# Seven products for eight in a projection of a hybrid decoder layer on eight cores

## The chip, the cores and the metric

The kernel runs on all 8 cores of one Trainium2 chip. Each core computes one prompt sequence of 2064 positions and 16 of the 128 sample tokens, 2080 tokens in all, with its own copy of the weights; the cores don't exchange anything. The metric is the device time of the slowest core in microseconds, as the median of several runs.

## The reference, cut to what matters

```python
def trunk_layer(x, ...):                       # x (B, T, 1024)
    h = rmsnorm(x, g_pre_mix)
    z = h @ w_in                               # 1024 -> 4096
    u, v, bg, cg, ga, gb = split(z)            # 512, 512, 512, 512, 1024, 1024
    a = multiscale_pool(u) @ w_pool * scale    # trailing means over 2, 4, 8, 16 tokens
    b = (bg * causal_dwconv(cg * v)) @ w_conv_out
    merged = sigmoid(ga) * a + sigmoid(gb) * b
    x = x + rmsnorm(merged @ w_o, g_post_mix)  # w_o: 1024 x 1024, the projection of the change
    h = rmsnorm(x, g_pre_ffn)
    gate, val = split(causal_dwconv(h @ w_up)) # 1024 -> 5632, 3 taps
    y = (silu(gate) * val) @ w_down            # 2816 -> 1024
    return x + rmsnorm(y, g_post_ffn)
```

The sample tokens go through the same layer with carried states (15 pooling rows, 2 convolution rows, 2 rows of the up-projection). All is float32 in DRAM; the matmuls take bfloat16 operands.

## The kernel before, in words

Activations lie transposed: channels on the 128 partitions, tokens along the free axis. Everything lies in one SBUF tensor `big`, and buffers are ranges of it that are used again by later stages. The first stage (mixer) cuts the 2080 tokens into five tiles, 512 and four times 392 (`TA`, index t = 0 to 4). The second (FFN) cuts them into 448, 464, 448, 448, 256 (`TB_N`).

For each mixer tile the kernel does, in program order: F, sixteen blocks of 8 matmuls for u, v, B and C (`F_block`, order `FSEQ`) with the convolution (`conv_c`, L666 and L669) and the pooling (`pool_c`, L697, L703) on VectorE; B, eight times two gates of 8 matmuls (`gates`, L804) and a merge of 1 + 4 matmuls (`merge`, L817, L821, L823), whose result is `MERGED[t]`; the projection `WO(t)`, eight groups of 8 matmuls with 392 columns, each evacuated by ScalarE twice (`wo_evac`: scaled by g_post_mix into `R[t]`, L834, and squared into `XSQ2[t]`, L836). Then `epi(t)`: a tree of additions (L602) and a matmul with ones give the mean square, ScalarE makes its inverse root (L611, L614); `epi_r` multiplies R by it (L864), adds x by an accumulating DMA issued from GpSimd (L570), squares (L872) and stores x to yT (L566, from SyncE's queue); `epi_n2` makes the second norm and `epi_x` (L888) writes h2, which goes to DRAM. `prenorm(t+1)` makes h of the next tile (L628, L640).

The work overlaps between tiles. Before the change the program order is B(0), WO(0), epi(0), B(1), then for t = 2 and 3: F(t), prenorm(t+1), WO(t-1), epi(t-1), B(t); then F(4) with WO(3) and epi(3) after its fifth block, B(4), WO(4). R, XSQ2, X and MERGED have one place each for all tiles (tile 0's are wider but begin at the same word), so a tile's R can be written only when its predecessor's readers, the products L888 and the yT stores, are through.

PSUM has 8 banks. Bank 7 is for norm sums, the other seven go round in program order (`next_bank`): a group of matmuls waits until the group seven banks earlier is evacuated.

The order on each engine is static. `Sched` records every operation with its tokens (ranges of SBUF in steps of 4 words, banks), keeps TensorE's in program order except the norm sums, and orders the other engines by a model of durations: the priority of an operation is the time at which TensorE's first operation that depends on it is due. The model gives each engine its own durations and knows of no influence of one engine's work on another's. All instructions then run in that order, with waits on semaphores. L559 issues every matmul.

The down-projection of the second stage already uses seven products for eight (`wdown`, with sums on GpSimd by `sumb`, L998, and bank additions on VectorE, L1056). `pre_ffn` prepares the sample tokens' share of the FFN convolution: a load of 704 KB and three products of 704 elements on GpSimd (L1190, L1192, L1194), in the period of tile 2.

## Time and profile before

| | |
|---|---|
| median of 3 runs | 798.0 us (797.36 to 799.73) |
| profiled execution, in all | 798.55 us |
| its span on the slowest core (core 2) | 797.0 us |
| spans of the 8 cores | 792.7 to 797.0 us |
| mean granted TensorE clock | 0.996 to 1.000 of 2.4 GHz |
| TensorE, VectorE, ScalarE, GpSimd busy | 98%, 73%, 55%, 41% |

A busy time is the union of an engine's instructions. Matmuls overlap in the pipeline and their ends are modelled, so the pace of a row of matmuls is the distance of their starts and not their duration. Times within the execution are counted in us from the start of the span. The mixer's periods, as far as the change touches them, lie at 144.8 to 205.4 us (F(2), WO(1), B(2)), 205.4 to 266.0 us (F(3), WO(2), B(3)) and 266.0 to 329.7 us (F(4), WO(3), B(4)); the last projection follows to about 338.5 us, and then the second stage begins.

### The profile page before, as it was taken

The numbers are of one execution on the slowest core, as the hardware profiler recorded it, in microseconds if no ns is written. First come the engines' busy times: TensorE is split into PE (matmuls) and PEld (weight loads), VectorE is DVE, ScalarE is ACT, GpSimd is POOL, SyncE is SP. The second block draws the span as 40 slices with busy tenths as digits, with TensorE's granted clock in tenths as the row PEclk, the third lists the DMA queues.
The fourth block names the chain that finished last, engine by engine and source line by source line (L and its number), as shares of the span: only waits on it lengthen the run. The fifth ranks groups of instructions, "written<-read, shape, count | busy, mean of one in ns | idle before, by whom it ended". The sixth has DMA issues, their size and how long they took to land.

```text
span 797.0 us, 16162 instructions; the slowest of 8 cores (792.7 to 797.0 us)
## 1 busy us (share of the span) xinstructions
PE 781.9 (98%) x4902; PEld 476.0 (60%) x4906; DVE 584.8 (73%) x1035; ACT 440.7 (55%) x998; POOL 326.0 (41%) x311
## 2 busy tenths in 40 slices
PE   6999999999999999999999999999999999999997
PEld 5445445555555555555554545577665777579984
DVE  1898438797886857578889839875679667885686
ACT  2433274675656545576676434754458534775562
POOL 6433001004001124559734312596556483494422
PEclk9999999999999999999999999999999999999999
DMA  9999813946303889999984787894535856258774
GB/s 181 196 164 151 131 52 98 211 100 156 117 22 67 194 150 196 175 149 159 127 194 159 146 145 240 273 186 149 172 109 77 193 179 186 60 109 253 232 226 155
DMA packets 82628, 124.35 MB, mean 156 GB/s; under 512 B 5584, under 2 KB 62544, under 8 KB 82528
## 3 DMA queue, kind: packets, MB, share of 16 engines
q0 software_dynamic: 38992, 43.14, 38.3%
q1 hardware_dynamic: 43552, 80.17, 33.5%
q8 instruction: 42, 0.69, 0.4%
q14 instruction: 42, 0.34, 0.2%
HBM read 117.40 MB, written 36.24 MB: 193 GB/s over the span
## 4 chain that ended last, share of the span: by engine, by line
PE 91%; DMA 3%; DVE 2%; issue 2%; ACT 1%; SPq 1%; DVEq 0%; ACTq 0%
PE ps L559 91%; DMA w_dns<-big 2%; DMA big<-xT 1%; DVE big L942 1%; SPq L566 0%; ACT big L938 0%; DVE big L1115 0%; DVE big L494 0%; DVE big L602 0%; ACT big L1228 0%; ACT big L628 0%; DVE big L1177 0%; DVEq L1390 0%; DVE big L759 0%; ACT ps L932 0%
## 5 line engine op out<-in xcount | busy, mean ns | idle before, releaser
L559 PE MATMUL ps<-big 128*128 128x392 bf16 (+10 forms) x4902 | 781.9, 323 | 9.9 <-ACT big L1228 4.7
L559 PEld LDWEIGHTS ps<-big 128*128 128x128 bf16 x4906 | 476.0, 98 | 315.4 <-issue 13.7
L942 DVE SCALAR_TENSOR_TENSOR big<-ps,big 128x448 f32<-128x448 f32 (+2 forms) x440 | 252.0, 636 | 85.1 <-ACT big L935 67.1
L952 POOL TENSOR_TENSOR big<-big 128x448 bf16<-128x448 f32 (+2 forms) x110 | 128.6, 1177 | 156.9 <-ACT big L951 102.3
L938 ACT ACTIVATE big<-ps,big 128x448 f32<-128x448 f32 (+2 forms) x220 | 126.9, 600 | 14.2 <-PE ps L559 5.4
L951 ACT ACTIVATE big<-big 128x448 f32<-128x448 f32 (+2 forms) x110 | 60.0, 546 | 67.2 <-DVE big L942 65.5
L998 POOL TENSOR_TENSOR big<-big 128x896 bf16<-128x896 bf16 (+3 forms) x45 | 87.9, 2010 | 20.5 <-PE ps L559 14.7
L570 POOL DMA_DIRECT2D big<-xT x16 | 15.3, 962 | 129.6 <-DVE big L817 116.8
L804 ACT ACTIVATE big<-ps 128x392 f32<-128x392 f32 (+1 forms) x80 | 38.9, 511 | 51.4 <-DVE big L823 26.7
L572 POOL DMA_DIRECT2D big<-w_up x44 | 31.4, 719 | 56.3 <-PE ps L559 51.5
L602 DVE TENSOR_TENSOR big<-big 128x1568 bf16<-128x1568 bf16 (+3 forms) x28 | 22.2, 794 | 38.6 <-ACT big L836 28.1
L932 ACT ACTIVATE ps<-big 128x4 f32<-128x4 f32 (+1 forms) x98 | 17.2, 175 | 53.8 <-PE ps L559 53.3
L817 DVE SCALAR_TENSOR_TENSOR big<-ps,big 128x392 f32<-128x392 f32 (+1 forms) x40 | 25.8, 644 | 27.5 <-PE ps L559 27.4
L572 POOL DMA_DIRECT2D big<-w_in x32 | 23.1, 733 | 21.1 <-DMA big<-w_in 11.5
L834 ACT ACTIVATE big<-ps,big 128x392 f32<-128x392 f32 (+1 forms) x40 | 24.3, 608 | 12.7 <-PE ps L559 12.6
L697 DVE TENSOR_TENSOR big<-big 128x406 f32<-128x406 f32 (+7 forms) x50 | 29.7, 596 | 1.5 <-ACT big L719 0.4
L1056 DVE TENSOR_TENSOR big<-big,ps 128x448 f32<-128x448 f32 (+1 forms) x48 | 28.1, 618 | 0.2 <-PE ps L559 0.2
L669 DVE SCALAR_TENSOR_TENSOR big<-big 128x392 f32<-128x392 f32 (+1 forms) x40 | 25.2, 642 | 2.9 <-ACT big L666 2.5
L640 DVE SCALAR_TENSOR_TENSOR big<-big 128x392 bf16<-128x392 f32 (+1 forms) x40 | 24.2, 646 | 3.7 <-ACT big L617 3.7
L888 DVE SCALAR_TENSOR_TENSOR big<-big 128x392 bf16<-128x392 f32 (+1 forms) x40 | 25.2, 674 | 1.5 <-ACT big L614 1.5
L872 ACT ACTIVATE big<-big 128x784 bf16<-128x784 f32 (+1 forms) x20 | 17.8, 892 | 14.8 <-DMA big<-xT 12.5
L823 DVE TENSOR_TENSOR big<-big 128x392 bf16<-128x392 f32 (+1 forms) x40 | 23.6, 599 | 1.9
(79 smaller groups left out, 423.2 us busy)
## 6 DMA issues: line engine op xcount, KB each, us to landing
big<-w_dns SPq DMA_DIRECT2D x30, 704.0 KB, 5.5
big<-w_up POOLq DMA_DIRECT2D x44, 256.0 KB, 13.5
big<-w_dnb SPq DMA_DIRECT2D x16, 704.0 KB, 5.1
big<-w_in POOLq DMA_DIRECT2D x32, 256.0 KB, 22.9
big<-xT POOLq DMA_DIRECT2D x16, 392.0 KB, 8.7
big<-w_dn POOLq DMA_DIRECT2D x8, 704.0 KB, 11.5
w_dnb<-big SPq DMA_DIRECT2D x8, 704.0 KB, 7.3
big<-xT SPq DMA_DIRECT2D x6, 784.0 KB, 7.2
```

Source lines behind the costliest of these rows:

```text
L559: ins = e.matmul(o, lhsT=l, rhs=x, start=(start and i == 0), stop=(stop and i == last))
L572: return S.add("pool", lambda e: e.dma_start(out=out, in_=in_, max_dma_last_dim=mx), r, w, dma=True, byts=byts, pri=pri, after=after)
L669: dve(lambda e, k=k: e.scalar_tensor_tensor(out=cv, in0=p[:, 2 + k + lo:2 + k + N], scalar=cc(C_WC + 4 * k + c), in1=cv, op0=ALU.mult, op1 ...
L697: dve(lambda e, nx=nx, cur=cur, s=s, a2=a2: e.tensor_tensor(out=nx[:, a2:W], in0=cur[:, a2:W], in1=cur[:, a2 - s:W - s], op=ALU.add), [ct] ...
L804: act(lambda e, b=b, g=g: e.activation(out=GT[t].ap[:, g, lo:N], in_=bank(b, N, lo), func=AF.Sigmoid), [("ps", b)], [GT[t].t(g, 1)], N, ps ...
L817: dve(lambda e: e.scalar_tensor_tensor(out=A_, in0=bank(bp, N, lo), scalar=cc(C_PS + m), in1=A_, op0=ALU.mult, op1=ALU.mult), [("ps", bp), ...
L938: act(lambda e, b=b, fj=fj, tt=tt: e.activation(out=tt[:, 0:n], in_=bank(b, n), func=AF.Copy, scale=cc(C_WF + fj)), [("ps", b), KCST], [to ...
L942: dve(lambda e, b=b, fj=fj, tt=tt, k=k: e.scalar_tensor_tensor(out=tt[:, 0:n], in0=ps[:, b * 512 + k:b * 512 + k + n], scalar=cc(C_WF + 44 ...
L951: silu[0] = act(lambda e: e.activation(out=g, in_=g, func=AF.Silu), [T.t(0, 1)], [T.t(0, 1)], n, tab="silu")
L952: prod[0] = S.add("pool", lambda e: e.tensor_tensor(out=gb.ap[:, q, 0:n], in0=g, in1=v, op=ALU.mult), [T.t()], [("sb", gb.off + q * gb.cw, ...
L998: pool_tt(lambda e, i=i, k=min(FH, i + 4): e.tensor_tensor(out=out[:, i:k, :], in0=gap(t, p0, h0)[:, i:k, :], in1=gap(t, p1, h1)[:, i:k, : ...
L1056: dve(lambda e: e.tensor_tensor(out=o, in0=o, in1=src, op=op), [("ps", b)] + tk, tk, N)
```

## The change

Tiles "2 to 4" of the change are t = 1, 2, 3. Write W for w_o in quarters (two halves of the input channels by two of the output channels) and M for MERGED in quarters (input channels by halves of the 392 tokens). `WO(t)` with its eight products of quarters becomes fourteen steps (`wo_step`: seven products A to G, two halves `md` of the output rows each). A step is 8 matmuls of 196 columns into one bank. F and G are copied out of the bank by ScalarE, twice each with opposite signs; the others are added to R in place by VectorE, once or twice. R is no longer scaled by g_post_mix in the evacuation; `epi_r` does it for t = 1 to 3 with eight products in place of four wider ones. The squares are taken from R after the last additions.

The steps are spread over F of the next tile (`F_with_WO`, table `WOAT`): from block 5 on in F(2), 3 in F(3) and 1 in F(4), the last four together after block 15 in F(2), two in F(3). The sums of M (five a tile, 784 elements, `wo_sum`) go to GpSimd. The sums of W are made once on chip by GpSimd (`wo_sums`, 21 instructions), partly in place of W's quarters, partly in gaps between buffers. As W's quarters B and E are overwritten, the last tile (`WO_last`) is computed from the sums F and G, the quarters D and C, and differences of MERGED's rows (eight subtractions on VectorE): as many matmuls of 392 columns as before, in another order, with four banks open at first in place of three.

To make room, `pre_ffn` moves to the second stage (third tile) in five chunks through the small buffer XB, each a load, three products on GpSimd and a store, and some buffers move by a few words.

```diff
@@
+    def wo_sums():
+        for o, p, q, op in (("F", "E", "C", ALU.add), ("G", "D", "B", ALU.add), ("B", "B", "C", ALU.subtract),
+                            ("A", "D", "C", ALU.add), ("E", "D", "E", ALU.subtract)):
...
+    MSUM = {"A": ((0, 0), (1, 1), ALU.add, MA), "B": ((1, 0), (1, 1), ALU.add, MB), "C": ((1, 0), (0, 0), ALU.subtract, (1, 0)),
+            "D": ((1, 1), (0, 1), ALU.subtract, MC), "E": ((0, 0), (0, 1), ALU.add, (0, 1))}
+    MRHS = {"A": MA, "B": MB, "C": (1, 0), "D": MC, "E": (0, 1), "F": (0, 0), "G": (1, 1)}
...
+    def wo_sum(t, p):
+        q0, q1, op, o = MSUM[p]
+        (a0, t0), (a1, t1) = mq(t, q0), mq(t, q1)
+        out, tk = mq(t, o) if isinstance(o, tuple) else (o.ap[:, :, 0:NA // 2], [o.t()])
+        pool_tt(lambda e: e.tensor_tensor(out=out, in0=a0, in1=a1, op=op), t0 + t1, tk, 2 * NA)
+
+    def wo_step(t, p, md):
+        h = NA // 2
+        r = MRHS[p]
+        rhs, rt = mq(t, r) if isinstance(r, tuple) else (r.ap[:, :, 0:h], [r.t()])
+        b = next_bank()
+        for mi in range(2):
+            w, wt = w_k(p, 2 * md + mi)
+            pe([(bank(b, mi * h + h, mi * h), w[k], rhs[:, k, :]) for k in range(4)], wt + rt, [("ps", b)], h)
...
+        for r2, half, op in {"F": ((4, 0, 1.0), (4, 1, -1.0)), "G": ((0, 1, 1.0), (0, 0, -1.0)),
+                             "A": ((0, 0, ALU.add), (4, 1, ALU.add)), "B": ((0, 0, ALU.add),),
+                             "C": ((0, 0, ALU.add), (4, 0, ALU.add)), "D": ((0, 1, ALU.subtract), (4, 1, ALU.subtract)),
+                             "E": ((4, 1, ALU.subtract),)}[p]:
+            o, tk = y(r2, half)
+            if p in "FG":
+                act(lambda e, o=o, op=op: e.activation(out=o, in_=src, func=AF.Copy, scale=op), [("ps", b)], tk, NA, psum=True)
+            else:
+                dve(lambda e, o=o, op=op: e.tensor_tensor(out=o, in0=o, in1=src, op=op), [("ps", b)] + tk, tk, NA)
...
+    WOSTEPS = [(p, md) for p in "FGBCDAE" for md in range(2)]
+
+    WOAT = {2: (5, 6, 7, 8, 9, 10, 11, 12, 13, 14, 15, 15, 15, 15), 3: (3, 4, 5, 6, 7, 8, 9, 10, 11, 12, 13, 14, 15, 15), 4: (1, 2, 3, 3, 4, 4, 5, 5, 6, 6, 7, 7, 8, 8)}
+
+    def F_with_WO(t):
+        for p in "BDA":
+            wo_sum(t - 1, p)
+        for i in range(16):
+            F_block(t, i)
+            if t == L and i < 9:
+                wup(1)
+            for x in [x for x, at in enumerate(WOAT[t]) if at == i]:
+                wo_step(t - 1, *WOSTEPS[x])
+                if x == 3:
+                    wo_sum(t - 1, "C")
+                    wo_sum(t - 1, "E")
+                if x == 13 and t == L:
+                    epi(L - 1)
+
+    def WO_last(hook):
...
+        ms = (4, 5, 6, 7)
+        bs = {m: next_bank() for m in ms}
+        for d, k0, k1 in ((0, 0, 4), (1, 0, 3), (1, 3, 4)):
+            for m in ms:
+                part(bs[m], m, d, k0, k1)
+        for m in ms:
+            wo_evac(t, bs[m], m)
+            hook()
...
@@
     epi(0)
+    wo_sums()
     B(1)
     load_states()
-    pre_ffn_load()
     for t in range(2, L):
-        for i in range(16):
-            F_block(t, i)
+        F_with_WO(t)
         load_x(t + 1, 2)
         prenorm(t + 1)
-        WO(t - 1)
         epi(t - 1)
-        if t == 2:
-            pre_ffn()
         B(t)
...
+    F_with_WO(L)
     small_states()
     B(L)
-    WO(L, split=True, hook=lambda: wup(1))
+    WO_last(lambda: wup(1))
     load_h2(0)
...
@@
+            if t == 2 and j % 4 == 1 and j < 20:
+                chunk = pre_ffn(j // 4)
+            if t == 2 and j % 4 == 3:
+                pre_ffn_sum(*chunk)
```

## Rows read from the trace of the kernel before

**Rows 1.** The page: the span, and busy time (share of the span) and count.

```profile
span 797.0 us, 16162 instructions; the slowest of 8 cores (792.7 to 797.0 us)
...
PE 781.9 (98%) x4902; PEld 476.0 (60%) x4906; DVE 584.8 (73%) x1035; ACT 440.7 (55%) x998; POOL 326.0 (41%) x311
```

**Rows 2.** Waits of TensorE, longest in total: in all, times, longest.

```profile
PE ps L559 <- ACT big L1228: 4.7, 2, 3.7
...
PE ps L559 <- DVE big L602: 1.3, 1, 1.3
```

**Rows 3.** Busy (x) of PE, PEld, DVE, ACT, POOL; then PEclk, DMA share, GB/s.

```profile
144.80:205.40 60.60, 60.60 (x367) 35.70 (x366) 49.04 (x86) 39.20 (x73) 8.55 (x7) 1.00 0.70 166
205.40:266.00 60.60, 60.60 (x367) 35.75 (x366) 45.83 (x82) 36.08 (x70) 3.49 (x4) 1.00 0.28 69
266.00:329.70 63.70, 63.03 (x381) 37.02 (x379) 48.07 (x103) 32.57 (x58) 22.12 (x32) 1.00 0.99 171
```

**Rows 4.** Groups by shape: busy us, mean ns of one, idle us before.

```profile
L559 PEld LDWEIGHTS ps<-big 128*128 128x128 bf16 x4906 | 476.0, 98 | 315.4 <-issue 13.7
L559 PE MATMUL ps<-big 128*128 128x392 bf16 x1464 | 245.2, 329 | 2.2 <-DVE big L602 1.3 <-ACT big L804 0.7 <-DVE big L778 0.2
...
L559 PE MATMUL ps<-big 128*128 128x224 bf16 x616 | 63.3, 259 | 0.0
```

**Rows 5.** Groups by shape, on ScalarE and VectorE.

```profile
L834 ACT ACTIVATE big<-ps,big 128x392 f32<-128x392 f32 x32 | 18.9, 591 | 12.7 <-PE ps L559 12.6
L640 DVE SCALAR_TENSOR_TENSOR big<-big 128x392 bf16<-128x392 f32 x32 | 18.8, 621 | 0.0
...
L821 DVE TENSOR_TENSOR big<-ps,big 128x392 f32<-128x392 f32 x32 | 17.9, 560 | 1.3 <-PE ps L559 0.8
```

**Rows 6.** Groups by shape: the sums on GpSimd.

```profile
L998 POOL TENSOR_TENSOR big<-big 128x896 bf16<-128x896 bf16 x20 | 38.3, 1923 | 12.8 <-PE ps L559 12.4
...
L998 POOL TENSOR_TENSOR big<-big 128x672 bf16<-128x672 bf16 x10 | 16.8, 1682 | 0.3
```

**Rows 7.** Timeline of VectorE: start, duration, instruction, idle before.

```profile
184.56 1.16 DVE L823 TENSOR_TENSOR big<-big 128x392 bf16<-128x392 f32 x1
...
188.25 0.55 DVE L821 TENSOR_TENSOR big<-ps,big 128x392 f32<-128x392 f32 x1
188.72 1.46 DVE L864 TENSOR_TENSOR big<-big 128x784 f32<-128x784 f32 x1
190.11 0.55 DVE L823 TENSOR_TENSOR big<-big 128x392 bf16<-128x392 f32 x1
190.59 0.96 DVE L864 TENSOR_TENSOR big<-big 128x784 f32<-128x784 f32 x1
```

**Rows 8.** Timeline of GpSimd at the same place.

```profile
183.91 1.37 POOL L1190 TENSOR_TENSOR big<-big 128x704 f32<-128x704 f32 x1 [42.67 <-PE ps L559]
185.43 1.53 POOL L1192 TENSOR_TENSOR big<-big 128x704 f32<-128x704 f32 x1
187.11 2.25 POOL L1194 TENSOR_TENSOR big<-big 128x704 f32<-128x704 f32 x1
```

**Rows 9.** Timeline of VectorE in F(2).

```profile
147.81 0.57 DVE L765 TENSOR_TENSOR big<-ps,big 128x392 f32<-128x392 f32 x1 [0.96 <-PE ps L559]
...
162.98 0.73 DVE L888 SCALAR_TENSOR_TENSOR big<-big 128x498 bf16<-128x498 f32 x1
...
165.28 3.97 DVE L888 SCALAR_TENSOR_TENSOR big<-big 128x498 bf16<-128x498 f32 x6
```

**Rows 10.** Timeline of SyncE's queue in F(2).

```profile
152.02 0.38 SPq L566 DMA_DIRECT2D yT<-big  x1
```

**Rows 11.** DMA issues at 151.5 to 165 us: count, KB, us to landing.

```profile
yT<-big SPq DMA_DIRECT2D x1, 996.0 KB, 9.5
```

**Rows 12.** Busy us of each engine near the start, with the granted clock.

```profile
8.00:12.80 4.80, 1.15 (x17) 0.88 (x15) 0.88 (x2) 1.06 (x1) 0.70 (x1) 0.96 1.04 206
12.80:16.20 3.40, 3.36 (x21) 2.37 (x22) 0.88 (x2) 1.06 (x1) 3.40 (x7) 0.56 1.12 228
```

More of the change, by code:

```diff
@@ L389, in build_nc @@
     al.o = o_sq2 + KC * NMX // 2
[L390 to L391 removed]
+    XB = Buf(SBW - 128 - 512, 8, 64)
+    al.o = XB.end
     ST_CONV = al(4, 2 * NS)
[L393 removed]
     X = per_tile(KC, False, [o_x, W_O.off] + [o_cv + 5 * NA + 32] * 3)
@@ L456, in build_nc @@
     PRE = Buf(h2b.off + 800, 44, NS)
-    PREW = Buf(ST_CONV.off - 44 * NS, 44, NS)
     H2, G = [h2a, h2b], [g0, g1]
-    ST_FFN = Buf(h2b.off, 44, 2 * NS)
-    assert ST_FFN.end <= PREW.off and PRE.end <= h2b.end <= ST_CONV.off
+    assert PRE.end <= h2b.end <= ST_CONV.off
     TAIL = Buf(h2b.off, 1, 44 * 18)
@@ new lines, in WO_last, with part @@
+    def WO_last(hook):
+        t, lo = NTA - 1, 0
+        mg = MERGED[t]
+        for i in (1, 0):
+            for k in range(4):
+                dve(lambda e, k=k, i=i: e.tensor_tensor(out=DB[i][k].ap[:, 0, :], in0=mg.ap[:, 4 * i + k, :], in1=mg.ap[:, 4 - 4 * i + k, :],
+                                                        op=ALU.subtract), [mg.t(k, 1), mg.t(4 + k, 1)], [DB[i][k].t()], NA, rate=2.0)
+        def part(b, m, d, k0, k1):
+            r = m // 4
+            w, wt = w_k(("DC" if d else "GF")[r], m % 4)
+            xs = [(DB[r][k].ap[:, 0, :], DB[r][k].t()) if d else (mg.ap[:, 4 - 4 * r + k, :], mg.t(4 - 4 * r + k, 1)) for k in range(4)]
+            pe([(bank(b, NA), w[k], xs[k][0]) for k in range(k0, k1)], wt + [xs[k][1] for k in range(k0, k1)], [("ps", b)], NA,
+               start=d == 0 and k0 == 0, stop=d == 1 and k1 == 4)
+        ms = (4, 5, 6, 7)
[6 more added lines that the diff above has]
+            hook()
+        for m in range(4):
+            b = next_bank()
+            part(b, m, 0, 0, 4)
+            part(b, m, 1, 0, 4)
+            wo_evac(t, b, m)
+            hook()
@@ L863, in epi_r @@
         r = R[t].ap[:, k:k + 2, lo:N]
-        tt(lambda e: e.tensor_tensor(out=r, in0=r, in1=SD.ap[:, rs, lo:N].unsqueeze(1).to_broadcast([128, 2, N - lo]),
-                                     op=ALU.mult), [R[t].t(k, 2), SD.t(rs, 1)], [R[t].t(k, 2)], 2 * N)
+        for x in range(k, k + 2) if 0 < t and not last else ():
+            dve(lambda e, x=x: e.scalar_tensor_tensor(out=R[t].ap[:, x, :], in0=R[t].ap[:, x, :], scalar=cc(C_G2 + x),
+                                                      in1=SD.ap[:, rs, 0:N], op0=ALU.mult, op1=ALU.mult),
+                [R[t].t(x, 1), SD.t(rs, 1), KCST], [R[t].t(x, 1)], N, stt=True)
+        if t == 0 or last:
+            tt(lambda e: e.tensor_tensor(out=r, in0=r, in1=SD.ap[:, rs, lo:N].unsqueeze(1).to_broadcast([128, 2, N - lo]),
+                                         op=ALU.mult), [R[t].t(k, 2), SD.t(rs, 1)], [R[t].t(k, 2)], 2 * N)
         if last:
@@ L1340, in build_nc @@
         if t == NTB - 1:
-            sp_dma(PRE.flat, pre_d, ["pre"], [PRE.t()], 128 * 44 * NS * 4, pri=-15000.0)
+            sp_dma(PRE.flat, pre_d, [("pre", 10 * c) for c in range(5)], [PRE.t()], 128 * 44 * NS * 4, pri=-15000.0)
         for j in range(FC):
```

94 lines of the change are left out of this document (63 added, 31 removed).

## The prediction

> **What bounds the kernel now.** I read the page's header and busy lines first, then the list of waits on TensorE, then the busy sums by stage, and last the timelines around two places. The page: TensorE is busy 781.9 of 797.0 us [rows 1], and its waits are 4.7 us behind the first evacuations at the start, and then single ones of up to 1.3 us [rows 2]. So the kernel is bound by the number of matmul columns: a column taken away is time gained, as long as no other engine becomes late. The next view says how near that is. In the three periods that the change touches (F of a tile, the projection before it, B of that tile) the sums show TensorE without a gap but for 0.67 us [rows 3], and VectorE busy 49.0 of 60.6, 45.8 of 60.6 and 48.1 of 63.7 us [rows 3]. Its room is 11.6, 14.8 and 15.6 us. GpSimd is nearly idle there, apart from DMA issues and the three state products that the change moves away.
>
> **The change part by part.**
>
> *Matmuls.* Matmuls overlap, so their mean duration is not their pace. A matmul of 392 columns lasts 329 ns; the period of 60.60 us holds 367, two of them cut by its edges, which is 166 ns each [rows 3, 4]. The difference, 163 ns, is the modelled end, so 224 columns (259 ns) go at 96 ns. That gives 0.417 ns a column, and 196 columns go at 84 ns. A projection was 64 x 0.166 = 10.6 us and becomes 14 steps x 8 = 112 x 0.084 = 9.4 us: 1.2 us less a tile, 3.5 us for tiles 1 to 3 (the diff's index). The last tile keeps 8 x 8 matmuls of 392 columns, so it gains nothing. Its first four banks finish together after 32 matmuls instead of three after 24, which moves ScalarE's evacuation, not TensorE. I cost that at 0, to at most 1 us if the differences come late behind the last merge.
>
> The Trainium skill speaks against this term: "TensorE: Matmul & The Clock Gate", section LDWEIGHTS, gives a weight load of 128 columns 128/1.2 = 107 ns. If loads set the pace, 112 of them would take 12.0 us, and three tiles would get slower by 4 us. The trace has a mean load of 98 ns [rows 4] and matmuls with a load each at 96 ns, so loads at least overlap down to that pace. Below it nothing is shown. If the pace stuck at 96 ns, the projection would take 10.8 us and the change would lose 0.4 us on three tiles; that is the bound I keep.
>
> *VectorE.* Added per tile: 2 x (2 + 1 + 2 + 2 + 1) = 16 additions of a bank (steps A to E), each like L821's 392 columns from PSUM. That one lasts 560 ns, but the next starts 0.48 us later (188.25 to 188.72) [rows 5, 7]: 7.7 us. The normalisation becomes 8 products like L640 (620 ns, about 0.54 apart) in place of 4 of 784 elements (about 0.9 apart): +0.8 us. So +8.5 us a period, while the period shrinks by 1.2. The room left is 1.9, 5.1 and 5.9 us. ScalarE loses 16 evacuations (591 ns for L834's [rows 5]) and gets 8 copies and 4 squares of double width, about as much: 0. The eight bf16 differences of the last tile are 8 x 0.3 to 0.5 us, beside TensorE's first 16 matmuls: 0.
>
> *GpSimd.* New: 20 weight sums of 512 elements (one in two pieces), and 5 sums of 784 elements a tile. L998 takes 1.68 us in the mean at 672 elements and 1.92 at 896, waits for VectorE within it included [rows 6]: I take 1.7 us for 784 and 1.2 for 512. F's and G's sums have only the weights and tile 0's freed buffers to wait for; B's and E's wait for the projection of tile 0, and A's for the squares of tile 0, whose room they take. So about 4 x 1.2 + 5 x 1.7 = 13.3 us of GpSimd fall into F of tile 2, 8.5 us into F of tiles 3 and 4, and 9.6 us into B of tile 1. GpSimd has the time. Behind a sum that waits for the last merge stand, in F of tile 4, issues of w_up loads, which are first used 232 matmuls (38 us) after F: 0. The question is what the sums do to VectorE. Three GpSimd products stand alone in the mixer, at 183.91, 185.43 and 187.11 us [rows 8]. The merge L823 beside the first, with two inputs in SBUF, took 1.16 us where its next takes 0.55, and L864 beside the third took 1.46 us where its next takes 0.96; L821, which reads PSUM, kept its 0.55 us beside the same product [rows 7]. So 5.2 us of GpSimd cost VectorE 1.1 us, where VectorE had gaps anyway. In F nearly two thirds of VectorE's work (convolution, pooling, h, h2, the trees) is of the kind with two SBUF inputs, and it runs without gaps. The bounds are 0.2 us of VectorE per us of GpSimd, as in these rows, and 1.0, if every sum meets a waiting instruction. I take 0.6, between them: nearer to the upper end than the row, since F has no gaps, and below it, since a third of the work is not of that kind. That costs VectorE 8.0 us in tile 2's period and 5.1 in each of the other two; 1.1 us comes back because the state products leave. The balance is 1.9 + 1.1 - 8.0 = -5.0, then 0.0 and +0.8 us.
>
> The Trainium skill, "SBUF", section Who interferes with whom, has the same thing as a rule: a VectorE instruction with two SBUF inputs and a GpSimd one that reads SBUF exclude each other, and the second waits for the whole of the first. By this rule, the trace agrees: L823 ended 0.4 us after the product did.
>
> *R and its readers.* The sums of tile t-1 are written into R by ScalarE (F and G) and added to by VectorE. R has one place for all tiles. Before, the projection came after all of F, so R had 21 us more to come free. Now F's first copy into rows 4 and 5 comes after block 5 of tile 2. F of tile 2 starts near 145.0: its second block ended when L765 started at 147.81 [rows 9], less two blocks of 1.33 us. Step F ends at 145.0 + 6 x 1.33 + 0.67 = 153.7. Seven banks rotate, two a block, so block 9 wants F's bank at 153.7 + 3 x 2.0 = 159.7. But the copy waits for the y store of tile 0's rows 4 to 7, issued at 152.02 and 9.5 us under way [rows 10, 11], and for the last products with h2's scale, which VectorE made from 162.98 to 169 us with nothing urgent behind them [rows 9]. The store alone puts the copy at 161.5 and block 9 at about 162.5 us: a wait of 3 us. ScalarE stands behind that copy too, with the v and u evacuations queued after it. This wait and VectorE's shortage of 5.0 fall together, since VectorE catches up while TensorE waits, and the banks let it be late by some 6 us. For tile 2 I take 3.5 us. Tiles 3 and 4 have the same reuse at blocks 3 and 1, with smaller stores behind: 0 to 2.5 us each, I take 0.75.
>
> *The rest.* The sample state's products move into the second stage: 15 small GpSimd products and 10 small DMAs over 20 pairs. That is the 5.1 us of the old ones spread out, on an engine busy 41% of the span [rows 1]; if a product of a pair comes later by 0.5 us, a bank's rotation covers it: 0. The h2 buffer moves by 64 words, and load_h2(1) now waits for the last projection: it is needed 22 pairs of 16 matmuls later. On SP nothing due sooner is behind it: 0, up to 1 us.
>
> **The sum.** -3.5 + 3.5 + 0.75 + 0.75 = +1.5 us. The profiled execution spans 797.0 and took 798.55 us in all; the median is 798.0. The forecast is 798.0 + 1.5 = 799.5 us. What this kernel's measurement can tell from no change is about 0.3%, 2.4 us: below 795.6 is faster, above 800.4 slower.
>
> **The rivals.**
> 1. *The columns come out whole* (0.22). The early copy is ordered well, R comes free sooner because its readers are now urgent, and GpSimd's price is the lower one, 0.2: balances 0.3, 3.4 and 4.2 us, all positive. Waits under 1.2 us in all; 794.5 to 795.7, best 795. For it: TensorE waits nearly nowhere before, with the same seven banks. Against: the store's landing is in the rows.
> 2. *VectorE becomes the bound* (0.25, the slower side). At 1.0 us per us, the balances are -10.3, -3.4 and -2.6 us, 16 us short; the banks and the work that can slip hide some of it once. Waits of 8 to 13 us, so 803 to 808 us, middle 805. It decides when GpSimd costs VectorE over 0.75 of its own time: then the second and third period are short too, by 1.3 and 0.5 us. For it: no gap in F; against: 0.2 in the only burst there. A gap in one piece can also cost clock: after a stretch in which TensorE was busy 1.15 of 4.8 us, the granted clock was 0.56 over the next 3.4 us [rows 12], which is 1.7 us more.
> 3. *Short matmuls don't go at 84 ns* (0.05). At 96 to 107 ns the columns give nothing or cost up to 4 us; with the waits above, 803 to 808.
>
> The forecast itself has 0.48, with waits of 2 to 8 us: 796.5 to 802.5. That the change doesn't do what it says has no part: the count of matmuls and columns stands in the diff.
>
> **How the numbers follow.** Faster: rival 1, 0.22. Slower by over 0.3%: rivals 2 and 3, and the upper quarter of the forecast's own case, 0.25 + 0.05 + 0.10 = 0.40. Within 0.3%: 0.38. The forecast's own range is 796.5 to 802.5; for 8 in 10 it reaches from 794.6 into rival 2's middle, 805.5.
>
> **What would show it.** Right: matmuls of 196 columns about 84 ns apart; in F of tile 2 a wait of TensorE for ScalarE or VectorE of about 3 us near 160 us; VectorE busy over 95% in F; its two-input instructions lengthened beside GpSimd's sums and the PSUM ones not. Wrong: if TensorE runs through F of tile 2 without a wait, rival 1 holds; if waits of several us stand in all three periods, rival 2.

## The result and the profile after

The changed kernel takes 814.95 us (814.06 to 817.02, 6 runs) against 797.72 us (6 runs) for the kernel before: 1.0217 times as long, 95% interval 1.0201 to 1.0233. That is 17.2 us slower. The forecast was 799.5 us, with a range from 794.6 to 805.5. Ratios and intervals, here and below, are of executions in which no die ran at a lowered clock.

The page of the changed kernel, on its slowest core (core 2); its lines answer to [rows 1].

```profile
span 815.5 us, 16715 instructions; the slowest of 8 cores (805.8 to 815.5 us)
...
PE 784.6 (96%) x5046; PEld 487.1 (60%) x5050; DVE 635.2 (78%) x1103; ACT 437.7 (54%) x993; POOL 379.9 (47%) x359
```

TensorE's busy time has hardly changed. What is new is waiting. The list of waits, for [rows 2] (columns: in all in us, times, longest in us); L922 is step F's copy into R, L819 the gates, L617 the trees, L877 the weight sums.

```profile
PE ps L574 <- ACT big L922: 10.4, 2, 5.3
...
PE ps L574 <- DVE big L617: 3.4, 3, 1.6
PE ps L574 <- ACT big L819: 2.6, 2, 1.7
...
PE ps L574 <- POOL big L877: 1.0, 1, 1.0
```

The three periods on the same core, for [rows 3], cut at the first matmul of F(2), F(3), F(4) and the last projection (columns as there):

```profile
145.90:210.70 64.80, 60.56 (x418) 38.95 (x416) 60.02 (x105) 35.91 (x67) 18.40 (x13) 1.00 0.50 101
210.70:278.60 67.90, 62.43 (x419) 40.07 (x417) 59.89 (x102) 36.16 (x67) 12.61 (x9) 0.95 0.32 81
278.60:346.10 67.50, 62.43 (x418) 40.47 (x417) 59.42 (x118) 30.75 (x53) 27.81 (x35) 0.95 0.77 139
```

They sum to 200.2 us; cut at the same matmuls, the kernel before took 184.0. The slowest core is not the typical one: in F(3) it waited 5.3 us in one piece, where the longest wait of the other seven was 1.2 to 1.9 us. Core 5 waited least of all, so what it shows is the part that the cores had in common. Its periods, and its waits between 110 and 345 us:

```profile
144.40:208.50 64.10, 60.71 (x417) 38.83 (x416) 60.57 (x105) 36.31 (x68) 20.39 (x13) 1.00 0.40 107
208.50:270.50 62.00, 60.32 (x418) 39.05 (x416) 59.05 (x102) 35.36 (x67) 12.74 (x9) 1.00 0.31 77
270.50:338.30 67.80, 62.74 (x418) 40.72 (x416) 59.34 (x118) 30.64 (x53) 27.72 (x35) 0.95 0.78 145
```

```profile
PE ps L574 <- ACT big L922: 7.8, 5, 5.1
PE ps L574 <- ACT big L819: 3.0, 3, 1.9
PE ps L574 <- DVE big L617: 0.2, 1, 0.2
```

And the 6.8 us around the end of its wait of 5.1 us, which ended at 285.7 us, on core 5, with TensorE's granted clock (the last column but two):

```profile
284.60:291.40 6.80, 5.68 (x28) 4.01 (x29) 6.39 (x13) 4.53 (x11) 0.24 (x1) 0.50 0.96 187
```

TensorE was granted half its clock for 6.8 us, from 1.1 us before the wait's end. It was busy 5.68 of them, so that costs 5.68 / 2 = 2.8 us. "The mixer", in all that follows, is the stretch from the first pair of 392-column matmuls behind 100 us to the first matmul of the second stage. That pair is a norm sum inside WO(0), some 7 us ahead of B(1). The account of core 5 over this stretch closes: measured from the distances of matmul starts, delays over 0.3 us are 12.4 us (the list above has 11.0 of them, as it leaves the first part of each wait out), half clock 2.8, fewer columns -3.5, together +11.7; the stretch is 239.9 us where the kernel before has 228.1, +11.8. On the other cores the delays, measured so, are 12.6 to 16.8 us; the median of the eight is 14.4.

Over the eight cores, as medians: the start up to that pair took 108.7 us before and 110.0 after, the mixer 228.1 and 241.4, the rest 457.2 and 458.9. So 13.3 us lie in the mixer; +1.3 and +1.7 lie ahead of it and behind it. These are medians of cores in one execution each, while the 17.2 us are of the slowest core over all executions, so they sum to 16.3 and not to 17.2.

Now the place of the longest wait, in F(4) on core 2. VectorE (start, duration, instruction, idle before), then GpSimd, ScalarE and TensorE:

```profile
284.61 3.44 DVE L684 SCALAR_TENSOR_TENSOR big<-big 128x392 f32<-128x392 f32 x1 [2.05 <-ACT big L681]
287.97 6.83 DVE L1017 SCALAR_TENSOR_TENSOR big<-big 128x392 bf16<-128x392 f32 x6
```

```profile
283.02 4.59 POOL L899 TENSOR_TENSOR big<-big 128x784 bf16<-128x784 bf16 x3
287.57 0.74 POOL L587 DMA_DIRECT2D big<-w_up  x1
288.33 1.68 POOL L899 TENSOR_TENSOR big<-big 128x784 bf16<-128x784 bf16 x1
289.94 0.74 POOL L587 DMA_DIRECT2D big<-w_up  x1
290.70 1.51 POOL L899 TENSOR_TENSOR big<-big 128x784 bf16<-128x784 bf16 x1
```

```profile
292.75 0.89 ACT L922 ACTIVATE big<-ps 128x392 f32<-128x392 f32 x2 [7.43 <-DVE big L1017]
```

```profile
293.77 6.47 PE L574 MATMUL ps<-big 128*128 128x196 bf16 x38 [5.07 <-ACT big L922]
```

L684 is a step of the convolution, 0.62 us elsewhere; L1017 are the products of tile 2's epilogue with h2's scale, the last readers of R, also 0.62 us each. One L684 took 3.44 us, and the first two L1017 2.47 and 2.28 us, because GpSimd's sums (L899) ran at that time: the last two of the row of three, and the two single ones behind it. Each ended some 0.43 us after a sum had ended: 288.05 after 287.61, 290.44 after 290.01, 292.65 after 292.21. The copy L922 into R had been possible for ScalarE since 285.3 us but for L1017, and ScalarE stood idle for 7.43 us; TensorE ran out of banks 5.1 us before it went on. On all eight cores of this kernel it is L1017, and never a store, that ends ScalarE's waits for R.

### The profile page after: what moved, and what is told of

Its sections match the earlier page's. It is cut to its first block, busy times and chain, and to the rows that moved or that the text cites. A ratio compares the mean times of both kernels' runs of the same rounds, so it can differ in the third digit from the quotient of the medians.

```text
span 815.5 us, 16715 instructions; the slowest of 8 cores (805.8 to 815.5 us)
## 1 busy us (share of the span) xinstructions
PE 784.6 (96%) x5046; PEld 487.1 (60%) x5050; DVE 635.2 (78%) x1103; ACT 437.7 (54%) x993; POOL 379.9 (47%) x359
## 4 chain that ended last, share of the span: by engine, by line
PE 72%; DMA 12%; DVE 6%; issue 6%; ACT 3%; POOL 1%; SPq 0%; DVEq 0%; ACTq 0%; POOLq 0%
PE ps L574 72%; DMA big<-xT 6%; DMA big<-w_o 3%; DMA w_dns<-big 2%; DVE big L1017 2%; DVE big L1071 2%; DMA h2T<-big 1%; DVE big L509 1%; ACT big L643 1%; DVE big L617 1%; POOL big L877 0%; ACT L626 0%; SPq L581 0%; POOL big L587 0%; DVE big L712 0%
## 5 line engine op out<-in xcount | busy, mean ns | idle before, releaser
L574 PE MATMUL ps<-big 128*128 128x392 bf16 (+11 forms) x5046 | 784.6, 319 | 25.7 <-ACT big L922 10.4
L574 PEld LDWEIGHTS ps<-big 128*128 128x128 bf16 x5050 | 487.1, 99 | 323.0 <-issue 36.9
L1081 POOL TENSOR_TENSOR big<-big 128x448 bf16<-128x448 f32 (+2 forms) x110 | 130.3, 1193 | 152.0 <-ACT big L1080 89.3
L819 ACT ACTIVATE big<-ps 128x392 f32<-128x392 f32 (+1 forms) x80 | 39.3, 513 | 54.2 <-DVE big L838 30.2
L585 POOL DMA_DIRECT2D big<-xT x16 | 15.6, 986 | 72.2 <-DVE big L989 55.4
L617 DVE TENSOR_TENSOR big<-big 128x1568 bf16<-128x1568 bf16 (+3 forms) x28 | 29.1, 1043 | 21.5 <-ACT big L851 13.9
L899 POOL TENSOR_TENSOR big<-big 128x784 bf16<-128x784 bf16 x15 | 26.8, 1802 | 36.0 <-DVE big L838 24.2
L877 POOL TENSOR_TENSOR big<-big 128x512 bf16<-128x512 bf16 (+2 forms) x21 | 25.4, 1228 | 35.4 <-DMA big<-w_o 18.7
L1017 DVE SCALAR_TENSOR_TENSOR big<-big 128x392 bf16<-128x392 f32 (+1 forms) x40 | 33.0, 879 | 0.8 <-ACT big L629 0.8
L587 POOL DMA_DIRECT2D big<-w_in x32 | 23.1, 735 | 20.0 <-DMA big<-w_in 11.1
L684 DVE SCALAR_TENSOR_TENSOR big<-big 128x392 f32<-128x392 f32 (+1 forms) x40 | 29.4, 744 | 2.3 <-ACT big L681 2.3
L655 DVE SCALAR_TENSOR_TENSOR big<-big 128x392 bf16<-128x392 f32 (+1 forms) x40 | 24.9, 666 | 4.0 <-ACT big L632 4.0
L509 DVE TENSOR_TENSOR big<-big 128x1408 bf16<-128x1408 bf16 (+2 forms) x30 | 25.1, 867 | 2.5 <-DMA w_dns<-big 2.5
## 6 DMA issues: line engine op xcount, KB each, us to landing
big<-w_dn POOLq DMA_DIRECT2D x8, 704.0 KB, 13.8
```

Of the source, the lines that this page charges most:

```text
L509: dve(lambda e, o=o, i0=i0, i1=i1, op=op, n=n: e.tensor_tensor(out=o.flat[:, 0:n], in0=i0, in1=i1, op=op), [x.t() for x in (bufs[r0], bufs ...
L574: ins = e.matmul(o, lhsT=l, rhs=x, start=(start and i == 0), stop=(stop and i == last))
L587: return S.add("pool", lambda e: e.dma_start(out=out, in_=in_, max_dma_last_dim=mx), r, w, dma=True, byts=byts, pri=pri, after=after)
L617: dve(lambda e, w=w: e.tensor_tensor(out=sq.ap[:, 0:w, 0:n], in0=sq.ap[:, 0:w, 0:n], in1=sq.ap[:, w:2 * w, 0:n], op=ALU.add), [sq.t(0, 2 * ...
L819: act(lambda e, b=b, g=g: e.activation(out=GT[t].ap[:, g, lo:N], in_=bank(b, N, lo), func=AF.Sigmoid), [("ps", b)], [GT[t].t(g, 1)], N, ps ...
L1017: dve(lambda e: e.scalar_tensor_tensor(out=h, in0=r, scalar=cc(C_G3 + k), in1=SD.ap[:, rs, lo:N], op0=ALU.mult, op1=ALU.mult), [R[t].t(k, ...
```

## The experiments

Theory L: GpSimd's sums cost VectorE its time, so that the epilogue of the tile before, which frees R, comes late and TensorE waits for the first copy into R. Theory R: the copies are due too early by their place in F, whatever GpSimd does. Each run is compared with runs of the kernel before on the same chip. The mixer's time is the median of the eight cores (228.1 us before, 241.4 after).

One thing has to be watched in every run that moves work. The planner orders VectorE by when TensorE needs a result, so an edit to the steps can also move the products L1017. The table has when the eight of them begin and end, in us behind the first matmul of F(3) and of F(4), as medians of the cores.

| kernel | F(3) | F(4) |
|---|---|---|
| before | 8.5 to 17.0 | 4.1 to 8.9 |
| changed | 12.1 to 19.1 | 9.4 to 17.8 |
| sums of MERGED on VectorE | 12.1 to 16.5 | 6.6 to 11.9 |
| all sums on VectorE | 12.0 to 16.4 | 7.0 to 12.3 |
| all sums on VectorE, later steps | 15.1 to 19.5 | 11.3 to 16.1 |
| sums on GpSimd, later steps | 14.5 to 21.7 | 14.4 to 22.0 |
| sums on GpSimd, chain first | 12.1 to 19.1 | 9.4 to 17.3 |
| sums held for all eight, later steps | 9.4 to 13.8 | 6.7 to 11.1 |
| sums held for all eight | 8.6 to 13.0 | 6.6 to 11.0 |

**The sums of MERGED on VectorE**

```diff
-        pool_tt(lambda e: e.tensor_tensor(out=out, in0=a0, in1=a1, op=op), t0 + t1, tk, 2 * NA)
+        dve(lambda e: e.tensor_tensor(out=out, in0=a0, in1=a1, op=op), t0 + t1, tk, 2 * NA, rate=2.0)
```

> The changed kernel with its 15 sums of MERGED's quarters on VectorE in place of GpSimd (the 20 weight sums stay on GpSimd). Theory L (GpSimd's sums block VectorE's two-input instructions, and that lateness makes the waits): VectorE gets 5 x 0.5 = 2.5 us of work a period and is spared some 6 us of lengthened instructions; the two waits of 5 us on the copies of step F in F(3) and F(4) shrink to under 2 us and the half clock behind them goes: 802 to 807 us. Theory R (the copies are simply due too early, since R's readers end where they end): the waits stay near 5 us, 812 to 816 us.

801.39 us, ratio 1.0045 (1.0029 to 1.0061); mixer 228.5 us. Of the 17.2 us, 13.6 are gone by moving fifteen instructions, a little more than theory L's range (802 to 807 us) has. Waits and groups by shape of this kernel (its L899 now on VectorE):

```profile
PE ps L574 <- ACT big L922: 1.7, 1, 1.7
```

```profile
L1017 DVE SCALAR_TENSOR_TENSOR big<-big 128x392 bf16<-128x392 f32 x32 | 19.4, 672 | 0.3 <-ACT big L697 0.3
...
L899 DVE TENSOR_TENSOR big<-big 128x784 bf16<-128x784 bf16 x15 | 9.0, 622 | 0.2
```

VectorE has nine us more of its own to do and still is early enough: L1017 is back at 672 ns from 863 in the changed kernel. The copies into R are due where they were, so their place alone is not what costs, and theory R falls. In none of its cores was the clock halved in the mixer.

**No sums of MERGED** (the seven products take quarters of MERGED as they are, so what they compute isn't the projection)

```diff
-    MRHS = {"A": MA, "B": MB, "C": (1, 0), "D": MC, "E": (0, 1), "F": (0, 0), "G": (1, 1)}
+    MRHS = {"A": (0, 0), "B": (1, 1), "C": (1, 0), "D": (1, 1), "E": (0, 1), "F": (0, 0), "G": (1, 1)}
```

> The changed kernel without the sums of MERGED's quarters: steps A, B and D read a quarter as it is, C and E too, so its output is not the reference's; matmuls, bank additions and weight sums are all there. Theory L: VectorE is spared the blocking and gets nothing instead, 799 to 804 us, and its two-input instructions in F keep their 0.57 to 0.97 us. Theory R: 811 to 815 us.

799.86 us, ratio 1.0025 (1.0012 to 1.0038), in theory L's range; mixer 226.5 us, 1.6 us under the kernel before. Even with the sums for nothing the change doesn't win in all, since the second stage took 2.3 us more here (459.5 against 457.2) and the start 0.8.

**The steps late** (all fourteen after block 15, in F(4) after block 4)

```diff
+    WOAT = {2: (15,) * 14, 3: (15,) * 14, 4: (4,) * 14}
```

> The changed kernel with all fourteen steps of a tile where the projection stood before (after block 15 of F(2) and F(3), after block 4 of F(4)); sums stay on GpSimd. Theory R: R is free long before, no wait on the copies of step F, 801 to 806 us. Theory L: VectorE has the same work and the same blocking; the waits go to the merges and sigmoids of B instead, 807 to 813 us.

818.92 us, ratio 1.0264 (1.0241 to 1.0287). Both theories missed, R by more. Its waits on the slowest core (core 0) are spread: 3.9 us between 140 and 345 us for the trees L617, 3.5 for the sums L899, 1.4 for the additions L924, and 6.6 in one piece for the copies L922, in F(4):

```profile
296.09 3.23 ACT L922 ACTIVATE big<-ps 128x392 f32<-128x392 f32 x8 [9.16 <-DMA yT<-big]
```

On this core and three others the store to yT was the last reader of R there, on the other four L1017. So R was late in F(4) though the copies were due three blocks later: the run moved its release too, and is no clean test of theory R.

**The kernel before with the same sums on GpSimd** (nobody reads them)

```diff
+        extra_sums(t - 1)
         for i in range(16):
             F_block(t, i)
```

> The kernel before with nothing but the same 15 sums of MERGED's quarters added on GpSimd at the same places (their results are read by nobody): the disputed cost by itself. Theory L: VectorE's busy time rises by 4 to 6 us in each of the three periods, its two-input instructions beside the sums last 1.2 to 2 us in place of 0.57 to 0.97, PSUM ones don't; its room of 11.6 to 15.6 us takes it up, so the time stays within 797 to 801 us. If GpSimd's sums cost VectorE only 0.2 of their time, busy rises by under 2 us a period.

799.80 us, ratio 1.0026 (1.0015 to 1.0037). By shape, GpSimd's sums and VectorE's L900 (the line that is L888 before, 660 ns there) and L669 (620 ns there):

```profile
L755 POOL TENSOR_TENSOR big<-big 128x784 bf16<-128x784 bf16 x15 | 26.4, 1788 | 19.5 <-DVE big L835 19.4
```

```profile
L900 DVE SCALAR_TENSOR_TENSOR big<-big 128x392 bf16<-128x392 f32 x32 | 28.5, 932 | 1.5 <-ACT big L614 1.5
L669 DVE SCALAR_TENSOR_TENSOR big<-big 128x392 f32<-128x392 f32 x32 | 23.7, 751 | 3.0 <-ACT big L666 2.5
```

L888 alone gained 32 x 0.272 = 8.7 us, L669 4.2, and the trees and the rest 2.8: 15.7 us of VectorE for 26.4 us of GpSimd, 0.59 per us. That is the prediction's 0.6, as a mean. By period it is not: VectorE's busy time rose by 3.4, 4.9 and 7.8 us (medians of the cores), while GpSimd's five sums took some 9.2, 9.7 and 7.9 us, so the price is 0.37, 0.51 and 1.0 per us. Theory L had 4 to 6 us in each. In the first two periods VectorE and GpSimd took turns: each waiting VectorE instruction ended about 0.4 us after a sum, and the sums behind the first ones took up to 2.2 us for their 1.5. In the third an L900 was held from 274.42 for 5.55 us, over three sums at their own 1.5 to 1.7 us. The kernel before gets 2.3 us slower by it, within the expected 797 to 801 us.

**Both loads in the kernel before**: the same sums, and after each block of F one addition of its bank into a spare buffer by VectorE (48 in all), the projection still behind F

```diff
+        if t > 1:
+            dve(lambda e: e.tensor_tensor(out=ACC.ap[:, 0, 0:NA], in0=ACC.ap[:, 0, 0:NA], in1=bank(b, NA), op=ALU.add),
+                [("ps", b), ACC.t()], [ACC.t()], NA)
```

> The kernel before with both of the change's loads but none of its early copies: the 15 sums of 784 elements on GpSimd (as in the run that had them alone, 799.8 us), and after each of the 16 blocks of F of tiles 2 to 4 one addition of its bank by VectorE into a spare buffer (48 additions of 392 columns, about 7.7 us a period), so that VectorE has as much to do as in the changed kernel. The projection stays behind F. Nothing reads the results. Theory L (the place of the first copy into R within F is part of the cause): banks are held a little longer, TensorE's waits stay under 4 us in all, 799 to 804 us. Rival (VectorE's shortage of time alone is enough): waits of 8 to 15 us, 807 to 815 us.

803.91 us, ratio 1.0073 (1.0057 to 1.0088); mixer 234.8 us, and the waits:

```profile
PE ps L559 <- DVE big L602: 5.4, 4, 1.9
```

So the two loads without the steps between the blocks make 6.7 us of the mixer's 13.3. The other 6.6 us came with the rest of the change: the steps, whose first copies want R early in F, the weight sums and the halved clock, which this kernel has on no core. How they divide isn't shown. Neither expectation fits whole: theory L's range holds the time, but the waits it had at under 4 us are 6.6 in the median core.

**All sums on VectorE**, the weight sums as well; and **only the weight sums** there

```diff
-                    pool_tt(lambda e, x=x, y=y, z=z, op=op, k=k: ...
+                    dve(lambda e, x=x, y=y, z=z, op=op, k=k: ...
```

> The changed kernel with both kinds of sums on VectorE, the 15 of MERGED and the 20 of the weights. Theory L (GpSimd's sums block VectorE's two-input instructions): the weight sums cost VectorE 20 x 0.4 = 8 us in place of 0.6 x 25 = 15 us, most of it where it has room (B(0), WO(0), B(1)); the waits of about 1 us in B(1) and B(2) that were left with only MERGED's sums moved go: 798 to 801 us. If GpSimd's weight sums had cost nothing, the 8 us added would show: 802 to 805 us.

> The changed kernel with only the 20 weight sums moved to VectorE; MERGED's stay on GpSimd. Theory L: the blocking beside MERGED's sums in F(3) and F(4) stays and with it the waits of about 5 us there; what falls before F(3) shrinks: 808 to 813 us. If the weight sums were the main cause, 800 to 805 us.

The first took 801.61 us, ratio 1.0061 (1.0044 to 1.0078), with the shortest mixer of all, 226.0 us: 2.1 us under the kernel before. Its time is outside both expectations and no better than with only MERGED's sums moved. The mixer is 2.5 us shorter than there, but the start is 1.4 us longer, and the execution with the profile was its fastest (799.66 us). The second took 817.77 us, ratio 1.0242 (1.0223 to 1.0261), above the 808 to 813 us of theory L: moving the weight sums alone gave nothing. The sums that matter are MERGED's.

**Later steps**: with all sums on VectorE, and with GpSimd's as in the change

```diff
+    WOAT = {2: (6, 7, 8, 9, 10, 11, 12, 13, 14, 14, 15, 15, 15, 15), 3: (6, 7, 8, 9, 10, 11, 12, 13, 14, 14, 15, 15, 15, 15), 4: (4, 4, 5, 5, 6, 6, 7, 7, 8, 8, 9, 9, 10, 10)}
```

> As the one before, and the fourteen steps begin later: after block 6 in F(2) and F(3), after block 4 in F(4) (up to block 10). Theory L with a remainder from the early use of R: the wait of 1.9 us on the copies of step F goes, 796 to 799 us. If the steps' crowding at the end of F makes VectorE late instead, 800 to 803 us.

> The changed kernel, all sums on GpSimd, with the steps beginning later as in the run before (block 6, 6 and 4). Theory R (due too early): the two waits of 5 us shrink to 1 to 2 us and the half clock goes, 803 to 808 us. Theory L: VectorE's lateness is only moved, waits in other places, 809 to 816 us.

809.13 us, ratio 1.0136 (1.0100 to 1.0171), and 817.09 us, ratio 1.0248 (1.0230 to 1.0266). Later steps help neither; without GpSimd's sums they cost 7.5 us. The first missed its expectation, and the second ended 1.1 us above theory L's range, 9 us above theory R's. But by the table the later steps made the planner put the products L1017 later too, by 3 to 4 us in the first kernel and by 2 to 5 in the second, so as a test of theory R they are not clean. In the F(4) of the first TensorE waited 5.1 us in one piece, and ScalarE's copies into R, once more the reason, waited for another reader of R this time, the store to yT:

```profile
282.87 3.23 ACT L922 ACTIVATE big<-ps 128x392 f32<-128x392 f32 x8 [5.74 <-DMA yT<-big]
```

The store was the last reader there on seven of the eight cores. So the release of R can be late even without GpSimd's sums, and then by the reader that the prediction had named.

**The epilogue's chain first**: its operations for tiles 1 to 3 planned 8 us earlier on every engine, in three kernels (sums of MERGED on VectorE; the changed kernel; all sums on VectorE)

```diff
+        S.boost = -8000.0 if 0 < t < L else 0.0
         epi_n1(t)
```

> The changed kernel with MERGED's 15 sums on VectorE (801.4 us, TensorE waits of 1.85, 0.84 and 0.33 us for step F's copies and their like), and in it the operations of the epilogue of tiles 1 to 3 (trees, inverse roots, products with R, products L1017) placed 8 us earlier in the priorities of VectorE, ScalarE and GpSimd, ahead of the next tile's normalisation and of the pooling. Theory L (what TensorE waits for is the latency of the epilogue's chain that frees R): two thirds of those waits go, 798.5 to 800.5 us. Rival (VectorE is short over the period as a whole, so the order can only move the wait): 800.5 to 803 us, with the waits in other places.

> The changed kernel (814.95 us) with the same earlier priorities for the epilogue's chain of tiles 1 to 3, all sums still on GpSimd. Theory L: the products L1017 end 2 to 4 us earlier, the two waits of 5.5 and 5.2 us for step F's copies shrink to 1 to 3 us each and the clock isn't halved behind them: 802 to 809 us. Rival (shortage over the period): the waits appear behind other instructions of VectorE, 812 to 817 us.

> The changed kernel with all sums on VectorE (801.6 us) and the epilogue's chain of tiles 1 to 3 placed 8 us earlier. Theory L: waits left are under 1 us, 798 to 801 us; if the order doesn't matter 801 to 803 us. Below 797.6 us it would beat the kernel before.

802.48 us (ratio 1.0052, 1.0038 to 1.0065), 813.82 us (1.0198, 1.0184 to 1.0212) and 801.53 us (1.0044, 1.0028 to 1.0060): the same as without it, within 1.2 us, and in the rival's ranges, not in theory L's. In the second, TensorE's waits for L922 are those of core 5 of the changed kernel:

```profile
PE ps L575 <- ACT big L923: 7.8, 5, 5.1
```

The second says less than it seems. Up to the end of L1017 in F(3), VectorE's order in it is that of the changed kernel but for merges and products with R in the B before, and in F(4) a tree and one evacuation change places: the chain stood about as early already, and the table has it end where it did, or 0.5 us earlier. So it doesn't test an earlier chain. In the first the chain did end 2.0 us earlier in F(3) and 0.9 us in F(4), and the mixer stayed at 228.5 us. This left open whether it is the coincidence with the chain or the lost time as such that counts.

**The sums held back** until the chain is through, with the steps two blocks later (F(3), F(4)) and with the steps in place. The first two kernels named one product L1017 as the end of the chain, which VectorE ran second, so that six of eight still ran beside sums; the next two named all eight.

```diff
-        pool_tt(lambda e: e.tensor_tensor(out=out, in0=a0, in1=a1, op=op), t0 + t1, tk, 2 * NA)
+        pool_tt(lambda e: e.tensor_tensor(out=out, in0=a0, in1=a1, op=op), t0 + t1, tk, 2 * NA,
+                after=[held[t - 1, k] for k in range(8)] if t > 1 else [])
```

> The changed kernel with GpSimd's MERGED sums of tiles 2 and 3 (in F of tiles 3 and 4) held until the last product L1017 of the tile before, so that none of them runs beside the chain that frees R, and the fourteen steps two blocks later there (from block 5 in F(3), block 3 in F(4)), so that the sums are in time. The number of sums, their engine and VectorE's work are as in the changed kernel (814.95 us), so the price per us of GpSimd stays. Theory L (VectorE's instructions wait through rows of GpSimd's sums just where R's release hangs on them): the waits of 1.4 to 5.2 us for step F's copies in F(3) and F(4) and the clock halved behind the latter go, what is left is up to 3 us behind late sums and crowded additions: 803 to 809 us. Rival (what counts is the time that VectorE loses in a period, wherever): 811 to 817 us.

> The same hold of the sums, with the steps where the changed kernel has them. Theory L: the waits for step F's copies go, and TensorE waits for the held sums in their place (step B is due at about 224 us in F(3) and 288 us in F(4), the held sum ends at about 228 and 291 us): two waits of 3 to 4 us named after GpSimd, 807 to 812 us. Rival (the period's loss alone): 812 to 817 us.

> As the run with the sums held and the steps later, but held until all eight products L1017 of the tile before are through: there the hold ended with the product of row 7, which ran second, and six of eight products still ran beside sums. Steps from block 5 in F(3) and block 3 in F(4). Theory L: no product L1017 is lengthened (0.6 us each), the waits for step F's copies and the clock halved behind them go, waits left in F(3) and F(4) are up to 2 us each behind late sums or additions: 803 to 809 us. Rival (the VectorE time that the sums cost over a period, wherever they run): 812 to 818 us, with the waits behind other VectorE instructions.

> The same full hold, steps where the changed kernel has them. Theory L: no wait for step F's copies over 1.5 us, but TensorE waits 2 to 4 us for the held sums in F(3) and F(4): 806 to 812 us. Rival: 812 to 818 us.

818.01 us (ratio 1.0253, 1.0235 to 1.0272), 815.61 us (1.0218, 1.0193 to 1.0242), 815.70 us (1.0213, 1.0190 to 1.0236) and 817.04 us (1.0231, 1.0207 to 1.0254). The first is above both ranges, the second, third and fourth are in the rival's. In the third the chain is clean, on its core 2 eight products L1020 (L1017 of the change) in 4.38 us, and by the table it ends 5 to 7 us earlier than in the changed kernel. But the sums then meet the convolution, and TensorE waits for them. VectorE, GpSimd, and the waits of TensorE:

```profile
279.53 4.38 DVE L1020 SCALAR_TENSOR_TENSOR big<-big 128x392 bf16<-128x392 f32 x8
283.82 2.23 DVE L686 SCALAR_TENSOR_TENSOR big<-big 128x392 f32<-128x392 f32 x4
285.98 0.56 DVE L782 TENSOR_TENSOR big<-ps,big 128x392 f32<-128x392 f32 x1
286.45 2.63 DVE L692 TENSOR_SCALAR big<-big 128x16 f32<-128x16 f32 x2
```

```profile
284.21 6.71 POOL L901 TENSOR_TENSOR big<-big 128x784 bf16<-128x784 bf16 x3
```

```profile
PE ps L576 <- POOL big L901: 5.2, 3, 3.1
PE ps L576 <- DVE big L619: 3.7, 3, 1.6
```

Three sums took 6.71 us here and 4.59 in the changed kernel, the row of four L686 having gone first. The waits for the copies are gone or down to 0.7 us in one piece on every core, as theory L said, and the time is the rival's. In both fully held kernels R comes free early, in the one with later steps the copies are due later as well, and TensorE still waits as long: delays of 16.4 and 15.6 us in the median core, against 14.4. What stayed is VectorE's loss. Over the three periods it is busy 179.1 us in the changed kernel, 178.0 and 180.7 in the fully held ones, 168.9 with MERGED's sums its own, and 161.1 without any (medians of the cores). So theory L is right about which instructions TensorE waited for in the changed kernel and wrong about why the time goes: the place of the sums only chooses who is late. In the changed kernel VectorE is busy 99, 99 and 92% of the time in F(2), F(3) and F(4) on core 5 (before, on the slowest core, 89, 89 and 70% of F and the projection); no stretch of F was found in which five sums fit without something being late.

## Why the prediction was wrong, point by point

- *What bounds the kernel.* Right, and VectorE's sums were not too small: it needed 179.1 us for the three periods, where the kernel before needed 141.8, +37.3 (medians of the cores); the prediction's terms give 3 x 8.5 + 18.2 - 1.1 = +42.6. VectorE's own additions and products, 25.5 there, are the term that was too large: the kernel without sums has 19.3 us more than the kernel before. The sums' share, 18.2 there, is 18.0.
- *Matmuls.* Right. The window 298.90 to 300.24 us in the changed kernel holds a row of 196-column matmuls, 16 starts on from the first in 1.34 us, 84 ns each:

```profile
298.90:300.24 1.34, 1.34 (x17) 1.33 (x16) 0.54 (x2) 0.50 (x1) 0.62 (x1) 1.00 0.29 75
```

  Core 5's account closes with -3.5 us. Rival 3 falls, and with it the rule of the Trainium skill, "TensorE: Matmul & The Clock Gate", section LDWEIGHTS, as a bound on the pace: 107 ns a load would have made the steps slower than what they replace.
- *VectorE's price.* 0.6 us per us of GpSimd was right as a mean (0.59). The reason given for it was not: VectorE did have gaps in F before, being busy 17.82 of 21.40, 19.70 of 21.30 and 13.82 of 21.30 us in the blocks of F(2), F(3) and F(4). And it was wrong in the third period, where 1.0 was measured in the kernel before with the sums. Wrong was also how it was used, as a debt that a period can pay back. It doesn't fall evenly: between 284.5 and 292.7 us VectorE got three instructions through, which take 0.53 us each without company. So it lost 6.6 of 8.2 us, in which GpSimd ran sums for 6.3 and issued DMAs in the rest.
- *R and its readers, and VectorE's shortage put at nothing for tiles 3 and 4*: the step that failed. For F(2) a wait of 3 to 3.5 us near 160 us was forecast; it is 1.2 us, near 162 to 167, on all cores but the slowest, which has 1.8 us for L617 at 155 instead. For F(3) and F(4) 0.75 us each was forecast, between 0 and 2.5, because the stores behind R are smaller there and the balances came out at 0.0 and +0.8 us. Measured on core 5: 2.2 us in F(3) and 5.2 in F(4); on the slowest core 5.5 and 5.2. In this kernel the store was the wrong reader. R comes free with the products L1017, and these stand at the end of a chain (tree, norm matmul, two ScalarE instructions, eight products) that ends 18 to 23 us after F has begun; the three first sums start in its midst, as soon as the last merge is through. That is the path by which the loss reached TensorE here. It is not the whole cause: with the chain kept clear of the sums TensorE waited as long in other places, and the time came back only when MERGED's sums left GpSimd (13.6 us).
- *The clock.* The prediction had a half-clock stretch only in rival 2, at 1.7 us. It came in F(4) on seven cores, for 3.4 or 6.8 us, and on the slowest also in F(3): 4.50 / 2 + 5.03 / 2 = 4.8 us there. In this kernel each of these stretches lies at a wait of TensorE of 3.3 us or more in one piece; on core 6 such a wait, 3.3 us, had none. In another kernel (all sums on VectorE, later steps) core 4 had 3.4 us of half clock where its longest wait was 2.2 us.
- *Costed at nothing.* The weight sums, and VectorE's lateness in B: waits of 1.05 us in B(1) and of up to 2.05 us in B(2) for the gates L819, on every core, neither in the kernel before. The first is the weight sums', since it is gone in both kernels that have them on VectorE. The second isn't theirs alone: 1.4 us of it are left with either kind moved, and it goes only when both are. The last tile: nothing, right; its projection takes 10.6 us in both. The second stage: 0 forecast, +1.7 us found, in all kernels of the changed form (458.6 to 460.4 as medians of the cores, and 457.4 in one) and not in the two of the form before (457.5 and 457.9). Where it appears, ScalarE waits at about 468 us for a store of weight sums (L1145 in the changed form, idle for 9.96 us in the kernel with all sums on VectorE); on SyncE's queue the planner has put seven stores of x in a row between two stores of weight sums there, where there were five before. But the slowest core of the kernel before has the same wait, 10.48 us idle at 467.69, and with it a delay of TensorE of 1.3 us; in the changed kernel the delays there are longer, up to 3.0 us. That the order of the stores is the cause is argued, not shown.
- *The rivals.* Rival 2, "VectorE becomes the bound", is what happened, with its mechanism. Its waits of 8 to 13 us were still too small: 12.4 on core 5, but 14.4 in the median core and 16.8 on the slowest. It gave 803 to 808 us, since it had the half clock only as an addition of 1.7 us (2.8 on core 5, 4.8 on the slowest) and nothing outside the mixer (3.0 us). Its condition, a price over 0.75, was met in the third period alone (1.0), not as a mean (0.59). It had 0.25, and the upper end of the range followed its middle.

## What to carry to other kernels

A balance of busy time over a period says whether an engine can do the work, not whether a result comes in time. Before work is put on GpSimd, find the chains that run while it does: each VectorE instruction with two inputs in SBUF can be made to wait for a whole row of GpSimd instructions, so multiply those of the chain by a GpSimd instruction's length, not by a mean. Then ask whether the other engine has the time at all: moving the sums away from the chain, without moving them off GpSimd, gave nothing here (815.7 and 817.0 us). Fifteen additions of 1.8 us on an engine that was nearly idle there cost 13.6 us; on the engine that was some 90% busy they took 0.5 us each and cost 2 us (mixer 228.5 against 226.5 us without them). And when an edit moves a due time, look where the planner has put the rest of the chain before calling the run a test.

## What was unexpected of the hardware

- A VectorE instruction that waits for GpSimd isn't always let in when one GpSimd instruction ends and the next begins. In F(2) and F(3) of the changed kernel it was, behind each sum. But in F(4) L684 began at 284.61, beside the second of three sums (283.02, 284.49, 286.13), and ended only 0.43 us after the third. What decides it isn't shown. The other way about, in the kernel with the sums held until all eight products were through, the first sum stood back for a row of four L686 and took 3.20 us, where 1.5 is its time without company. The Trainium skill, "SBUF", section Who interferes with whom, has it that the first to issue holds the port for its whole instruction; the trace agrees for one instruction, and shows that a holder can keep it over a row.
- The length of a VectorE instruction doesn't matter for that: L692, L694 and L696, with 16 elements and 0.22 us alone, took 1.0 to 2.0 us beside the sums. Instructions that read PSUM kept their 0.55 us everywhere (L924: 554 ns in the mean of 48).
- Eight cores that run the same program don't wait in the same places: in F(3) one had 5.5 us in one wait and the others 1.4 to 2.0 in the longest of several. The page of the slowest core alone would have put F(3) beside F(4) as a cause; on the other seven the waits of F(4) are the larger ones.
